# Second output gate and branch input as seven block products each, weight sums on GpSimd, silus behind the state copies

## The reference

```python
p = jnp.einsum('bld,de->ble', h, w_in)
u, q, k, v, g, gates, lr = jnp.split(p, IN_SPLITS, axis=-1)
...
y_pool = ... pooled(u) ...
o = chunked gated linear attention(q, k, v, log decays from lr)
y_gla = jnp.matmul(rmsnorm(o) * jax.nn.silu(g), w_gla_br)
gate_pool, gate_gla = jnp.split(jax.nn.sigmoid(gates), 2, axis=-1)
x = x + g1 * jnp.matmul(gate_pool * y_pool + gate_gla * y_gla, w_o)
```

## Time and profile before

| what | value |
|---|---|
| median of 3 runs | 1620.58 us (1620.1 to 1623.28) |
| profiled execution: its own time | 1623.43 us |
| profiled execution: span of its instructions | 1621.6 us |
| TensorE's mean granted clock | 0.985 of full speed |
| stretch of the change | about 127 to 195 us |

### The profile page before, as it was taken

One profiled execution on the slowest core, in us unless ns is written; L12 is line 12 of the kernel. 1 busy time (PEld: TensorE's weight loads), 2 busy tenths in 40 slices (PEclk: granted clock), 3 DMA queues, 4 the chain that ended last, 5 costly groups with the idle time before them and its releaser, 6 DMA issues.

```text
span 1621.6 us, 29895 instructions
## 1 busy us (share of the span) xinstructions
PE 1546.7 (95%) x12718; PEld 1250.9 (77%) x12718; DVE 874.1 (54%) x1562; ACT 370.4 (23%) x688; POOL 157.1 (10%) x204
## 2 busy tenths in 40 slices
PE   6999999999999986788899999999999999999998
PEld 4459889964544543444789899999999889999998
DVE  2779987641110100000289737877557964587854
ACT  3125221120000100000234332233022443223311
POOL 0400000032000000000222101100202210110020
PEclk9999999999999998889999999999999999999999
DMA  9844364989999999999644114544444313345550
GB/s 364 303 171 156 109 232 180 390 347 411 425 427 426 429 424 426 428 414 415 213 167 144 56 53 131 182 157 158 181 125 156 105 54 105 104 156 174 185 189 27
DMA packets 126580, 376.86 MB, mean 232 GB/s; under 512 B 15386, under 2 KB 64898, under 8 KB 111232
## 3 DMA queue, kind: packets, MB, share of 16 engines
q1 hardware_dynamic: 125076, 374.23, 60.3%
q0 software_dynamic: 1216, 0.89, 0.2%
q10 hardware_dynamic: 172, 0.05, 0.0%
HBM read 374.10 MB, written 1.05 MB: 231 GB/s over the span
## 4 chain that ended last, share of the span: by engine, by line
PE 82%; DMA 10%; DVE 5%; ACT 1%; issue 1%; SPq 1%; DVEq 0%; ACTq 0%
PE PS L1880 15%; PE PS L784 11%; DMA ring<-in_moe_w_dram 8%; PE PS L1285 7%; PE PS L1977 6%; PE PS L906 5%; PE PS L1314 3%; PE PS L1577 3%; PE PS L1837 3%; PE PS L972 3%; PE PS L1231 2%; PE PS L1996 2%; PE PS L1382 2%; PE PS L1238 2%; PE PS L1488 2%; PE PS L947 2%
## 5 line engine op out<-in xcount | busy, mean ns | idle before, releaser
L1880 PE MATMUL PS<-arena,ring 128*128 128x128 f32 x2240 | 252.9, 275 | 1.7 <-ACT arena L2795 0.9
L1880 PEld LDWEIGHTS PS<-arena,ring 128*128 128x128 f32 x2240 | 251.3, 192 | 2.4 <-ACT arena L2795 1.3
L3979 DVE TENSOR_TENSOR ring<-ring 128x1024 f32<-128x1024 f32 x112 | 137.9, 1250 | 2.4 <-DMA ring<-in_ffn_w_up_dram 0.9
L784 PE MATMUL PS<-arena,ring 128*128 128x256 f32 x576 | 126.4, 380 | 0.0
L784 PEld LDWEIGHTS PS<-arena,ring 128*128 128x128 f32 x576 | 108.7, 190 | 16.4 <-issue 1.0
L1977 PE MATMUL PS<-arena,ring 128*128 128x128 f32 x896 | 101.0, 275 | 0.0
L1977 PEld LDWEIGHTS PS<-arena,ring 128*128 128x128 f32 x896 | 100.5, 192 | 0.0
L3491 DVE COPY arena<-PS 128x512 f32<-128x512 f32 (+1 forms) x16 | 11.0, 690 | 142.0 <-PE PS L1382 91.6
L4000 DVE SCALAR_TENSOR_TENSOR arena<-arena,colsL 128x255 f32<-128x255 f32 (+1 forms) x160 | 76.4, 519 | 2.3 <-ACT arena L2782 0.2
L1382 PE MATMUL PS<-ring,arena 128*32 128x512 f32 x256 | 40.4, 785 | 38.4 <-DMA ring<-in_moe_w_dram 37.8
L3471 DVE TENSOR_TENSOR arena<-arena,PS 128x512 f32<-128x512 f32 x8 | 8.5, 1057 | 99.1 <-PE PS L1285 99.1
(11 more groups left out here) (599 smaller groups left out, 2614.8 us busy)
## 6 DMA issues: line engine op xcount, KB each, us to landing
ring<-in_moe_w_dram SPq DMA_DIRECT2D x58, 2048.0 KB, 17.8
arena<-in_moe_w_dram SPq DMA_DIRECT2D x24, 2048.0 KB, 18.9
ring<-in_w_in_dram SPq DMA_DIRECT2D x22, 2048.0 KB, 9.2
ring<-in_ffn_w_up_dram SPq DMA_DIRECT2D x44, 1024.0 KB, 7.2
ring<-in_ffn_w_down_dram SPq DMA_DIRECT2D x10, 2048.0 KB, 8.1
ring<-in_moe_w_dram SPq DMA_DIRECT2D x12, 1024.0 KB, 9.5
ring<-in_w_mod_dram SPq DMA_DIRECT2D x16, 512.0 KB, 12.2
ring<-in_w_mod_dram SPq DMA_DIRECT2D x8, 1024.0 KB, 9.7
```

Of the source, the lines that this page charges most:

```text
L784: last = mm(PS[:, b, place] if not isinstance(place, tuple) else PS[place[0], b, place[1]], lhsT(k), rhs(k), start=(k == 0), stop=(k == K ...
L1880: last = mm(PS[:, b, th(i)], w4[:, k, th(i)], b4[:, k, :], start=(first and i == 0 and k == 0), stop=(end and i == 1 and k == 3), skip_gro ...
L3979: V.tensor_tensor(to[n - 1], a, b_, op).then_inc(S("weights_summed"), 1)
```

## The change

g1 and u become units of `seven_project`. Their weight sums, u's token sums 2 to 4 (g1 reads the same ones; the first is q's `first_sum`), gate0's four token sums and its first two weight sums are made by GpSimd, in the order of the block at the end of the diff, counted by a new semaphore `late_sums`. g1's sums lie where q's did (`qdki`), so GpSimd begins them after q's seventh product. u is split: "one" and "two" stand ahead of krc, the other five behind. The silus of g, before part of the copies out of PSUM, are now two instructions of 128x1024 behind the state copies. Several PSUM banks are named by hand.

```diff
-SEVEN = (("q", 0), ("g", 0), ("gate", 0), ("gate", 1), ("gate", 2), ("gate", 3), ("gbr", 0), ("gbr", 1))
...
+SEVEN = (("q", 0), ("g", 0), ("g", 1), ("u", 0), ("gate", 0), ("gate", 1), ("gate", 2), ("gate", 3), ("gbr", 0), ("gbr", 1))
+BY_POOL = {(("g", 1), 1): 4, (("g", 1), 2): 5, (("g", 1), 3): 6, (("g", 1), 4): 7,
+           (("u", 0), 3): 8, (("u", 0), 1): 9, (("u", 0), 2): 10, (("u", 0), 4): 11, (("gate", 0), 1): 12, (("gate", 0), 2): 13}
+BY_VECTOR = [(key, n) for key in SEVEN for n in range(1, 5) if (key, n) not in BY_POOL]
+AHEAD = {"part_sums": 2 * TT, "sum_products": 28 + 7 * len(SEVEN), "weights_summed": 12 + len(BY_VECTOR), "tokens_summed": 16,
...
+            ("g", 1): qdki_parts,
+            ("u", 0): [qdki_parts[1], qdki_parts[3]] + thousands(flat(s0)),
...
+            "u": [first_sum, hboth[:, 4:8, 0:P], hboth[:, 4:8, P:T], lrT.rearrange("p (k c) -> p k c", k=4)],
...
+        fifth = {("q", 0): early_fifth, ("g", 0): early_fifth,
+                 ("g", 1): wlr.rearrange("p k c -> p (k c)").rearrange("p (i c) -> p i c", i=2),
...
+        def wait_sum(eng, key, n):
+
+            if (key, n) in BY_POOL:
+                eng.wait_ge(S("late_sums"), BY_POOL[(key, n)])
+            else:
+                eng.wait_ge(S("weights_summed"), 5 + BY_VECTOR.index((key, n)))
+
+        def wait_tokens(eng, key, n):
+
+            if key[0] in ("gate", "u") or key == ("g", 1):
+                if key[0] != "gate" and n == 1:
+                    eng.wait_ge(S("tokens_summed"), 5)
+                else:
+                    eng.wait_ge(S("late_sums"), 13 + n if key[0] == "gate" else n - 1)
+            else:
+                eng.wait_ge(S("tokens_summed"), (8 if key[0] == "gbr" else 4) + n)
...
             seven_project("g", 0, banks=(1, 2, 3))
-            project("g", 1, "g", hx)
+            seven_project("g", 1, banks=(4, 5, 6))
...
                     for t in range(TT):
-                        b = ph1.bank(pe, (name, d, t))
+                        b = ph1.bank(pe, (name, d, t), 2 + 2 * d + t)
...
+            seven_project("u", 0, SEVEN_STEPS[:2], banks=(7, 1, 6))
             by_token("krc", (e1, e2), 1)
-            project("u", 0, "u", hx)
+            seven_project("u", 0, SEVEN_STEPS[2:], banks=(7, 1, 6))
...
-                         lambda t, h=2 * hp + i: vtok[:, t, h * 256:(h + 1) * 256]) for i in range(2)], TT)
+                         lambda t, h=2 * hp + i: vtok[:, t, h * 256:(h + 1) * 256]) for i in range(2)], TT,
+                          bank=2 + 2 * d + hp)
...
-                b = ph1.bank(pe, ("sc", h))
+                b = ph1.bank(pe, ("sc", h), (1, 5, 6, 7)[h])
...
-                    b = ph1.bank(pe, ("kv", h, n), 1 + n)
+                    b = ph1.bank(pe, ("kv", h, n), (2, 3, 4, 1)[n])
...
-                b = ph1.bank(pe, ("o", h), 5)
+                b = ph1.bank(pe, ("o", h), 7)
...
+                copies = (("A", 1, seven_place(key, 0, 0)), ("A", 3, seven_place(key, 0, 1)), ("D", 4, fifth_of(key)),
...
                 A(ki[:, d], cum[:, d, :, T:2 * T], ACT.Exp, scale=-inv).then_inc(S("qdki_exp"), 1)
 
-            silu_of_first_g()
+            seven_last(("g", 0), ACT.Copy)
...
-            log_exp_table()
+            seven_copies(("g", 1))
             for d, e in ((0, e1), (1, e2)):
                 act.wait_ge(S("krc_arg"), d + 1)
                 A(e, e, ACT.Exp, scale=inv).then_inc(S("key_decays"), 1)
+            seven_last(("g", 1), ACT.Copy)
             act.wait_ge(S("decays"), 1)
             A(dec, lastx, ACT.Exp, scale=inv).then_inc(S("dec_ready"), 1)
             decays_of(0)
-            nc.scalar.preload_act_table_set("silu_and_others")
-            silu_of_g(1)
-            log_exp_table()
+            seven_copies(("u", 0), range(3))
...
+            seven_copies(("u", 0), range(3, 4))
             act.wait_ge(S("cumb_ready"), 1)
+            wait_sum(act, ("u", 0), 4)
             decays_of(1)
             A(e2, e2, ACT.Exp, scale=inv).then_inc(S("key_decays"), 1)
...
+            seven_last(("u", 0), ACT.Copy)
...
+            nc.scalar.preload_act_table_set("silu_and_others")
+            for j in range(2):
+                for bank in "BDA":
+                    ph1.freed(act, (bank, ("g", j)))
+                A(sg[:, 4 * j:4 * j + 4, :], sg[:, 4 * j:4 * j + 4, :], ACT.Silu)
...
+            seven_added(("g", 1))
...
+            seven_added(("u", 0))
+            dve.wait_ge(S("sum_products"), seven_products(("u", 0), 7))
             mod_rows(2, MOD_SLABS[0])
-            seven_tokens_summed(("gate", 0), range(1, 5))
-            seven_weight_sums(("gate", 0), range(1, 3))
...
+            def late_tokens(key, ns):
+
+                to = tokens_of(key)
+                for n in ns:
+                    if n % 2 == 0:
+                        wait_tokens(pool, key, n - 1)
+                    a, b_ = ((seven_rows("g", 0, 1), seven_rows("g", 0, 0)), (seven_rows("g", 1, 1), to[0]),
+                             (seven_rows("g", 1, 1), seven_rows("g", 0, 1)), (seven_rows("g", 1, 0), to[1]))[n - 1]
+                    nc.gpsimd.tensor_tensor(to[n - 1], a, b_, ALU.subtract).then_inc(S("late_sums"), 1)
...
+            def late_weights(key, ns):
...
+                for n in ns:
+                    if n == ns[0]:
+                        pool.wait_ge(wl[i % 3], before1[i % 3] + 16 * (i // 3 + 1))
+                    if n % 2 == 0:
+                        wait_sum(pool, key, n - 1)
+                    if n == 4:
+                        wait_sum(pool, key, 2)
+                    a, b_, op = ((a21, a22, ALU.add), (to[0], a11, ALU.subtract), (a11, a21, ALU.subtract),
+                                 (a12, to[1], ALU.subtract))[n - 1]
+                    nc.gpsimd.tensor_tensor(to[n - 1], a, b_, op).then_inc(S("late_sums"), 1)
+
+            ph1.read(pool, "lr")
+            late_tokens(("u", 0), range(2, 4))
+            ph1.read(pool, ("z", 1, GH - 1))
+            late_tokens(("u", 0), range(4, 5))
+            pool.wait_ge(S("sum_products"), seven_products(("q", 0), 7))
+            late_weights(("g", 1), range(1, 5))
+            pool.wait_ge(S("sum_products"), seven_products(("g", 0), 7))
+            late_weights(("u", 0), range(3, 4))
+            pool.wait_ge(S("sum_products"), seven_products(("g", 1), 6))
+            late_weights(("u", 0), (1, 2, 4))
+            pool.wait_ge(S("krx_arg"), 1)
+            pool.wait_ge(S("qdki_exp"), 2)
+            late_weights(("gate", 0), range(1, 3))
+            pool.wait_ge(S("keys_decayed"), 4)
+            late_tokens(("gate", 0), range(1, 5))
```

More of the change, by code:

```diff
@@ L419, in seven_place @@
             o = 4 * key[1] + 2 * v
+            if key[0] == "u":
+                return hboth[:, 2 * v:2 * v + 2, th(t)]
             if key[0] == "q":
@@ L777, in _, with tiles @@
             mm = nc.tensor.matmul
-            def tiles(ph, key, parts, K, start=0):
-                b = ph.bank(pe, key)
+            def tiles(ph, key, parts, K, bank=None):
+                b = ph.bank(pe, key, bank)
                 for place, lhsT, rhs in parts:
@@ L3020, in seven_added @@
                     else:
-                        link(V.tensor_tensor(place, place, fifth[key[0]], ALU.add))
+                        link(V.tensor_tensor(place, place, fifth_of(key), ALU.add))
             v_added("vA", 9, 3, 2, 1, False)
@@ L3167, in _ @@
             token_squares(GH - 1).then_inc(S("otok_steps"), 1)
-            for g in range(2):
-                ph1.freed(dve, ("u", 0, g))
+            ph1.freed(dve, ("A", ("u", 0)))
             ph1.read(dve, ("o", GH - 1))
```

66 lines of the change are left out of this document (26 added, 40 removed).

## The result

| | us | against before |
|---|---|---|
| before, median of 4 | 1621.12 (1620.1 to 1623.28) | |
| changed, median of 4 | 1644.68 (1643.23 to 1645.62) | ratio 1.0133, interval 1.0121 to 1.0145 |
| changed, profiled execution | 1645.62, span 1643.8 | span of before 1621.6 |

The kernel became slower by 1.2 to 1.45%. The ratio applied to 1620.58 gives 1642.1 us, just inside the range that was stated; the median itself, 1644.68, lies 1.7 us above its upper end. The forecast of 1636.0 was a loss of 15.4 us; measured were 23.6 and, in e8, 20.2. So the direction and the mechanism came out, and the loss was forecast 5 to 8 us too small.

A forecast was written before the change was run, and what follows sets the result against it. PE was taken to bound the stretch, DVE having almost no slack. DVE's 19.0 of holding - 1.5 - 5.05 + 2.5 = +15.0 us delays PE by 15.6: 1620.6 + 15.6 = 1636.2, forecast 1636.0, range 1622 to 1643.

The forecast's parts named there:

- What bounds the kernel, and that the loss reaches the end.: From 120 to 300 us PE bounds, DVE has almost no slack, and any loss there reaches the end whole.
- PE's part.: Seven products for g1 and u save PE 2.64 us, less 0.4 for a bank wait: 2.2 us gained if sums are free.
- ACT's part at nothing.: ACT's moved silus and copies lie in its idle time before the row at 185.23 and cost zero.
- The price of a turn, 2.17.: Each 128x1024 GpSimd sum delays DVE's two-operand SBUF work by 2.37 - 0.2 = 2.17 us.
- "Less 1.5 of idle time.": DVE's idle time before its row at 132.43 was to take 1.5 us off the 19.0 of holding.
- "4.2 of the 6.2 ahead of the keys.": Of 6.2 us holding by three of u's sums, 4.2 delay krc's keys, whose second half ends at 164.5.
- +15.6 us at the second group of scores.: PE's second scores wait for DVE's last krx copy, starting at 194.5 instead of 178.87: 15.6 us later.
- "Behind, PE's pace is as before.": After the waits at krc and the second group of scores, PE goes on at its old pace, nothing added.
- Hidden sums: Rival: GpSimd's sums cost DVE nothing and PE's 2.6 us arrive, giving 1618.4 us; chance 0.15.
- Half turns: Rival: scans and sums overlap in part, 1.1 us a sum, DVE +5.55, giving 1626.8 us; chance 0.15.
- All held: Rival: each sum holds DVE for its whole length, +24.8 us on DVE, giving 1646 us; chance 0.05.

The follow-up runs named there:

- e8: The changed kernel measured again, unedited, beside the kernel before: 1641.99 us, ratio 1.0126.
- e1: The changed kernel with each of GpSimd's seventeen late sums cut to one column in 128 or 256: 1620.23 us, 0.9984 of before.
- e9: The changed kernel with product two of u made five times ahead of krc and head 0's scores nine times: 1639.66 us, 1.0114 of before.
- e3: The kernel before with thirteen useless GpSimd memsets, which write SBUF and read nothing: 1621.54 us, 0.9998 of before.
- e2: The kernel before with thirteen useless GpSimd subtractions of constants in SBUF: 1638.58 us, 1.0101 of before.

## Why the prediction was right, and where it was short

**What bounds the kernel, and that the loss reaches the end.** Right. DVE had no slack at krc: 13.8 us of lateness at the keys (165.90 against 152.13) became 7.85 of waiting there, and e1, which takes only the sums' length away, loses both waits. The 19.46 us of lateness at the state updates are still there at 760 us, and the whole kernel is 22.2 us longer.

**PE's part.** Right: 2.2 us were to be won with free sums, and e1 measured 2.1 (0.16%, 0.06 to 0.25).

**ACT's part at nothing.** Right as to the moved silus. ACT's copies did make PE wait (1.2 and 0.8 us), because DVE was late with what ACT waited for; the next wait on DVE took that up.

**The price of a turn, 2.17.** Right within its bounds, a little high in the mean (2.02). Held instructions were longer by 2.16 (L3038), 2.04 (scan at 136.95), 1.98, 1.97, 2.02 and 1.95. By groups, working against trace:

| group | worked out | measured, from which rows |
|---|---|---|
| u's token sums 2 and 3 | 0 | 0.4 (128.81 against 127.99 of before is 0.82 late, 0.38 of it from the start) |
| g1's four | 5.2 | 5.0 (the addition behind the first scan starts 5.84 late, at 140.25, and 0.82 before them) |
| u's third | 2.1 | 2.0 (142.57) |
| u's first, second, fourth | 6.2 | 5.95 (155.26, 157.95, 161.23) |
| gate0's two | 3.0 | 3.0 (176.35 by 2.03, 180.72 by 0.97) |
| gate0's four token sums | 2.5 | 2.3 (186.57, 188.33, 190.29 by 0.96, 0.57, 0.80) |
| sum | 19.0 | 18.7 |

**"Less 1.5 of idle time."** This step failed, the first of two that made the forecast too small. The row at 135.68 still has 1.52 us of idle time ahead of it, as the one at 132.43 had: ACT's logarithms wait for DVE's own inputs, so the idle time moved with DVE and absorbed nothing. With 18.7 + 0 - 5.05 + 2.3 (the six additions by their pitch) DVE should be 15.9 late; it is 16.3, 0.4 of which this execution had from its start.

**"4.2 of the 6.2 ahead of the keys."** All three of u's sums fell ahead of them, and the idle time wasn't absorbed: the second half of the keys ended at 168.2, not 164.5. PE itself was ready for krc at 159.3, 3.5 us later than worked out (mostly the two waits for ACT's copies, 1.2 and 0.8 us, and the 0.8 us that it was behind from q on), so its wait was 7.85, near the 7.5 for the wrong reason. Nothing followed, since the next wait was on the same engine.

**+15.6 us at the second group of scores.** 17.02 measured (16.6 without the later start). The difference of 1.0 is the 1.5 us of idle time that was not there, less 0.5 by which the holding and the additions were priced too high.

**"Behind, PE's pace is as before."** This step failed too. The prediction had waits of 7.5 and 10.7 us in PE's list and nothing for the clock behind them. It fell both times; the first fall was absorbed, the second cost 2.4 us (e9 wins 2.33 back). 15.6 + 1.04 + 2.44 = 19.1 us of lateness; the two measurements by medians are 20.2 (e8) and 23.6. What is above 19.1 is not tied to a cause: the profiled executions differ by up to 3 us through stretches of low clock behind 340 us, and the changed kernel and e8 have the further 1.4 us between 862 and 883.

**The rivals.** Hidden sums are out (e3 against e2: the same places and shapes, and only the reading ones hold DVE). Half turns are out: scans are held like adds. All held is out: DVE's copies ended 16.3 us late and not 24.8. That its 1646 lies near the first median of 1644.68 is chance, since the clock and not DVE made up the difference.
